# Gate and up of the small experts in two products of a joint high-low tile and a fold

## The chip, the cores and the metric

The kernel runs on one core of a Trainium2 chip. The metric is the device time of one execution in microseconds; the time before is the median of three runs. All times below are microseconds unless marked ns.

## The reference, cut to what matters

A two-layer hybrid block (latent attention, retention, block attention, then a dense feed-forward in layer 0 and eight routed experts in layer 1) is followed by a second block (feed-forward, gated mixing, cross attention, feed-forward), all in float32, on 256 tokens of width 1024. The change lies in the eight experts:

```python
def swiglu(x, w_gate, w_up, w_down):
    return (jax.nn.silu(x @ w_gate) * (x @ w_up)) @ w_down

def moe_swiglu(x, w_router, w_gate, w_up, w_down):      # D_MODEL 1024, D_FF_EXPERT 3584, N_EXPERTS 8, TOP_K 2
    ...
    y = jnp.zeros((B * S, D), jnp.float32)
    for e in range(N_EXPERTS):
        y = y + gates[:, e:e + 1] * swiglu(xt, w_gate[e], w_up[e], w_down[e]).astype(jnp.float32)
    return y.astype(x.dtype).reshape(B, S, D)
```

## The kernel before, in words

TensorE multiplies in a shortened float32 (fp32r). To keep float32 accuracy, every operand is split into a high part and a low part, and a product is made of three: high by high, high by low, low by high (`mm3`, L653 to L655). The weights come as a stream of chunks of 128 x 2048 float32 (1 MB). SyncE loads chunk n into one of six places of `raw` as soon as VectorE has split the chunk that stood there; ScalarE copies it to `whi` (the high part, `hi`, L1616); VectorE subtracts to get `wlo` (`lo`, L2134). `whi` and `wlo` have three homes each (`SPLIT`), so `hi` of chunk n waits until TensorE has used chunk n-3 (semaphore `used`).

In the expert stage each expert has the tokens that chose it, gathered as rows. Experts are sorted by their number of tokens; those at places 2, 4 and 6 (`FEW`) have at most 64 rows and are called small here, the others large. An expert's hidden width of 3584 is cut into 14 units of 256. A **slot** is one unit's gate and up (two chunks, 8 k-steps of 512 columns: 256 of gate and 256 of up) and the down projection (one chunk) of the slot before it, so down runs one slot late. Places 1 to 6 are worked in pairs: slots alternate between a large and a small expert. So 42 of the 112 slots are small ones.

In the texts below the three chunks of a small slot are **a** and **b** (gate and up of the small expert, k-steps 0 to 3 and 4 to 7) and **c** (down of the large unit before); those of a large slot are **d** and **e** (gate and up of the large expert) and **f** (down of the small unit before). A pair of slots is a b c d e f. Before the change, a, b, c, d and e take 12 products of 512 columns each, f takes 8: down of a small unit (`down_few`, L967 and L969) already uses a joint tile, with the high parts of 64 rows in columns 0 to 63 and the low parts in columns 64 to 127 of one 128-column operand, so that two products do for three and leave two halves of 64 rows that are added when the expert's sums are taken out (L1783, L1784 on ScalarE, L2403, L2405 on VectorE).

The order of the work on each engine is written out by hand:

- TensorE (`slot` in `experts`): gate and up of the slot, with two transposes of the former slot's gated unit (`turn`, L992) after k-step 1; in some slots four transposes that bring a later expert's rows into its lane (`turn_rows`, L940); then down of the former slot.
- ScalarE (`slot`): `hi` of the next slot's first chunk; wait for the end of gate and up; Silu of the gate half (L1796, written to `prob`); the lane copy (L1776) in gathering slots; `hi` of the next two chunks; the high part of the turned unit (L1814, `hth`).
- VectorE (`slot`): `lo` of the next slot's first chunk; gate by up (L2440); lane differences (L2395); `lo` of the next two chunks; the low part of the turned unit (L2461 for a small, L2464 for a large one, semaphore `e_ht`), for which down waits.

So `hi` and `lo` run for the slot ahead: during a large slot (d, e, f) they make a, b and c of the next small slot, and during a small slot d, e and f.

The lanes: a large expert's rows stand in `xth` (high) and `xtl` (low), a small expert's in `mem_hi` and `mem_lo`, the two halves of `mem_t`, 128 columns each, of which half are used. Slots whose code repeats were run in loops (`LOOPED`) on TensorE, ScalarE and VectorE.

Of the kernel before, what the change touches and what calls it, by code (L numbers as in the profile page):

```python
# [24 lines left out]
P = 128  # L25
# [32 lines left out]
SLOTS_FEW = P // 2  # L58
RANK_AT = (0, 1, 5, 2, 6, 3, 7, 4)
MIXED_AT = 8  # L60
GU_BANKS, TURNED_BEHIND = (0, 5), 1


def slot_of(e, j):

    if e == 0 or e == NE - 1:
        return U_E * e + j
    return U_E * (2 * ((e - 1) // 2) + 1) + 2 * j + (e - 1) % 2


SLOT = sorted(((e, j) for e in range(NE) for j in range(U_E)), key=lambda u: slot_of(*u))
GATED_AT, GATES_TURN_AT, X_SCALED_AT = slot_of(0, 6), slot_of(0, 8), slot_of(1, 7)
SHARES_AT, ROWS_BACK_AT = (slot_of(1, 6), slot_of(1, 8)), slot_of(1, 9)
GATHERS = {slot_of(0, 6): (1, 0), slot_of(0, 9): (1, 1), slot_of(0, 11): (2, 0), slot_of(0, 13): (2, 1)}
# [2 lines left out]
    for _g in range(2):  # L77
        GATHERS[slot_of(_beside, _j + _g)] = (_e, _g)
LOOPED = {slot_of(0, 2): 2, slot_of(NE - 1, 2): 2}
for _e in range(1, NE - 1, 2):  # L80
    LOOPED.update({slot_of(_e, 2): 3, slot_of(_e, 11): 2})
NEG = -1e30


# [193 lines left out]
def program(nc, stream, x_in, mem_in, pos_in, consts, route_in, cols_in, rows_in, ws_in, blank_in, out):  # L278
    with ExitStack() as ctx:
# [127 lines left out]
        def pair_columns(p, part, slot=0, heads=2):  # L407

            a = C_PAIR + W_PAIR * p + 2 * HD * part + HD * slot
            return slice(a, a + HD * heads)  # L410

        landed = [sem(f"landed{n}") for n in range(RAW)]
        hi_done = sem("hi_done")
        lo_done = sem("lo_done")
# [1 line left out]

        def lane(e):

            hi, lo = (mem_hi, mem_lo) if e in FEW else (xth, xtl)
            q = (e // 2 - 1) % 2 if e in FEW else (e + 1) // 2 % 2  # L420
            return hi, lo, slice(q * P, (q + 1) * P)

        def f32(ap):
            return ap.bitcast(F32)
# [225 lines left out]
        def _(pe):  # L650
# [270 lines left out]
            def experts():  # L921
# [18 lines left out]
                        m = pe.transpose(ps[4][:, k * P:(k + 1) * P], xs[:, (4 * g + k) * P:(4 * g + k + 1) * P], ident)  # L940
                    m.then_inc(sem("e_ga"), 1)

                def gate_up(e, bank, a, b, turned=None, first=False):
                    xh, xl, mine = lane(e)
                    for j, c in enumerate((a, b)):
                        chunk(c)
                        if first:
                            pe.wait_ge(sem("e_gx"), j + 1)
                        wh = whi[:, c.split, :].rearrange("p (k n) -> p k n", k=4)
                        wl = wlo[:, c.split, :].rearrange("p (k n) -> p k n", k=4)  # L950
                        for k in range(4):
                            kk = 4 * j + k
                            m = mm3(ps[bank][:, :], xh[:, kk, mine], xl[:, kk, mine],
                                    wh[:, k, :], wl[:, k, :], start=(kk == 0), stop=(kk == 7))
                            if kk == TURNED_BEHIND and turned is not None:
                                turn(turned)
                        m.then_inc(used, 1)

# [51 lines left out]
                def slot(s, it=0):  # L1010

                    e, j = SLOT[s]
                    u, base = s + 2 * it, first_chunk - 1 + 3 * s
                    if s == 0:
                        gate_up(e, GU_BANKS[0], Chunk(first_chunk), Chunk(first_chunk + 1), first=True)
                        return
                    if j == 0:
                        pe.wait_ge(sem("e_gx"), 2 * (e + 1))
                    if s == GATES_TURN_AT:
                        turn_gates()  # L1020
                    gate_up(e, GU_BANKS[s % 2], Chunk(base, it), Chunk(base + 1, it), u - 1)
                    if s in GATHERS:
                        if GATHERS[s] == (1, 1):
                            pe.wait_ge(sem("rt_spread"), 1)
                        turn_rows(*GATHERS[s])
                    done, n = SLOT[s - 1]
                    if n == 0 and done > 0:
                        pe.wait_ge(sem("e_oa"), done)
                        pe.wait_ge(sem("e_od"), done)
                    if s == 1:  # L1030
                        pe.wait_ge(*at("wk", "ev", 4))
                    if s == U_MOE - 1:
                        down(Chunk(base + 2), u - 1, done % 2, False, False, halves=(0,))
                        turn(u)
                        down(Chunk(base + 2), u - 1, done % 2, False, False, halves=(1,))
                        return
                    (down_few if done in FEW else down)(Chunk(base + 2, it), u - 1, done % 2, n == 0, n == U_E - 1)

                pe.wait_ge(sem("rt_one"), 1)
                pe.wait_ge(*at("wk", "ev", 2))  # L1040
                for g in range(2):
                    gather_first(g)
                keys(FILL["gather"])
# [558 lines left out]
        def _(act):  # L1602
# [167 lines left out]
            def experts():  # L1770
                first_chunk = AT["f1"]

                def gathered(e, g):
                    act.wait_ge(sem("e_ga"), 2 * e + g + 1)
                    xh, _, mine = lane(e)
                    act.activation(xh[:, 4 * g:4 * g + 4, mine], ps[4 + g if e == 0 else 4][:, :].rearrange("p (k s) -> p k s", k=4),  # L1776
                                   ACT.Copy).then_inc(sem("e_gh"), 1)

                def outputs(e, q, done):
                    act.wait_ge(sem("y_kept"), e + 1)  # L1780
# [7 lines left out]
                def slot(s, it=0):  # L1788

                    e, j = SLOT[s]  # L1790
                    few, final = e in FEW, s == U_MOE - 1
                    u, base = s + 2 * it, first_chunk - 1 + 3 * s
                    n = base + 3
                    hi(Chunk(n, it))
                    act.wait_ge(used, base + LB * it + 2 + (s == 0))
                    act.activation(sg[:, 0, :], ps[GU_BANKS[s % 2]][:, 0:FU], ACT.Silu).then_inc(sem("e_sg"), 1)  # L1796
                    if s == X_SCALED_AT:
                        act.wait_ge(sem("xg_in"), 16 * 2 * T)
                        for t in range(T):
                            act.activation(x[:, t, :], x[:, t, :], ACT.Copy, scale=float(ALPHA)).then_inc(sem("x_scaled"), 1)  # L1800
                    if s == GATES_TURN_AT:
                        act.wait_ge(sem("rt_turned"), 1)
                        act.activation(spread, ps[4][:, 0:S], ACT.Copy).then_inc(sem("rt_spread"), 1)
                    if s in GATHERS:
                        gathered(*GATHERS[s])
                    if final:
                        hi_half(Chunk(n + 1), 0)
                    else:
                        for i in (1, 2):
                            hi(Chunk(n + i, it))  # L1810
                    act.wait_ge(sem("e_ut"), u + 1)
# [10 lines left out]
                act.sem_inc(sem("e_oa"), 1)  # L1822
                for g in range(2):
                    gathered(0, g)
                advance(first_chunk + LEAD - 1)
# [290 lines left out]
        def _(dve):  # L2116
# [272 lines left out]
            def experts():  # L2389
                first_chunk = AT["f1"]  # L2390

                def gathered(e, g):
                    dve.wait_ge(sem("e_gh"), 2 * e + g + 1)
                    xh, xl, mine = lane(e)
                    dve.tensor_tensor(xl[:, 4 * g:4 * g + 4, mine], ps[4 + g if e == 0 else 4][:, :].rearrange("p (k s) -> p k s", k=4),  # L2395
                                      f32(xh[:, 4 * g:4 * g + 4, mine]), ALU.subtract).then_inc(sem("e_gx"), 1)

                def outputs(e, q, done):
# [30 lines left out]
                def slot(s, it=0):  # L2429
# [5 lines left out]
                    if final:  # L2435
                        lo_half(Chunk(n), 0)
                    else:
                        lo(Chunk(n, it))
                    dve.wait_ge(sem("e_sg"), u + 1)
                    dve.tensor_tensor(hs[:, 0, :], sg[:, 0, :], ps[GU_BANKS[s % 2]][:, FU:2 * FU], ALU.mult).then_inc(sem("e_h"), 1)  # L2440
                    if s in GATHERS:
# [10 lines left out]
                    if final:  # L2452
                        lo_half(Chunk(n), 1)
                    else:
                        for i in (1, 2):
                            lo(Chunk(n + i, it))
                    dve.wait_ge(sem("e_hh"), u + 1)
                    cut = slice(P, 2 * P) if final else slice(0, P)
# [784 lines left out]
```

## Time and profile before

| | |
|---|---|
| median of 3 runs | 2002.49 us |
| lowest and highest | 2001.07 and 2004.5 us |
| the profiled execution's own time | 2005.42 us |
| its span, first to last instruction | 2003.6 us |
| mean granted clock of TensorE | 0.996 |
| share of the span: PE, PEld, DVE, ACT, POOL | 98%, 81%, 75%, 62%, 4% |
| large and small slots in turn | from about 621 to 1298 us |

PE is TensorE, PEld its weight loads, DVE VectorE, ACT ScalarE, POOL GpSimd, SP SyncE. PE's busy share counts a product from its start to its modelled end; products overlap in the array, so that they start about 0.23 us apart although each lasts 0.39. An engine's row in the timeline gives the start, the length, the line and, in brackets, for how long the engine was idle before it and what released it.

### The profile page before, as it was taken

To read this page: it belongs to the slowest core of one execution; us is meant where nothing else is said; L and a number is where in the kernel's file an instruction comes from. 1 tells how busy PE (TensorE), PEld (TensorE's weight loads), DVE (VectorE), ACT (ScalarE), POOL (GpSimd) and SP (SyncE) were. 2 spreads that over 40 slices of the span, in tenths; PEclk is the share of its full clock that TensorE was granted. 3 is DMA by queue.
4 is the path that set the end of the run, shared out by engine and by line. 5 is a ranking of instruction groups with operands and counts; after the bars stand their busy time and mean duration, and the time that the engine had idled before them with its cause. 6 is when DMAs were issued, how large, how long until landed. Compare 5 with 4: busy or idle time off the path is not lost.

```text
span 2003.6 us, 25756 instructions
## 1 busy us (share of the span) xinstructions
PE 1959.0 (98%) x9454; PEld 1629.3 (81%) x9454; DVE 1502.3 (75%) x1573; ACT 1236.5 (62%) x1330; POOL 76.5 (4%) x96
## 2 busy tenths in 40 slices
PE   7999999999999999999999999999899999999998
PEld 6978887889788877888887888888688889888886
DVE  6685546777899989999999999999865556655554
ACT  5555444565777777777777777777644455535443
POOL 0002000001000000000000000010000012000000
PEclk9999999999999999999999999999999999999999
DMA  8348553436999999999999999999655545345550
GB/s 334 119 143 300 208 198 139 166 133 237 364 376 391 394 382 383 392 409 385 401 391 401 401 381 390 391 414 410 243 210 188 189 159 184 142 149 185 187 187 26
DMA packets 79663, 555.15 MB, mean 277 GB/s; under 512 B 8976, under 2 KB 9104, under 8 KB 17632
## 3 DMA queue, kind: packets, MB, share of 16 engines
q1 hardware_dynamic: 73728, 523.01, 68.1%
q0 software_dynamic: 5840, 30.85, 4.1%
q8 instruction: 63, 1.03, 0.2%
q14 instruction: 32, 0.26, 0.0%
HBM read 544.91 MB, written 12.58 MB: 278 GB/s over the span
## 4 chain that ended last, share of the span: by engine, by line
PE 90%; DVE 6%; ACT 2%; issue 1%; DMA 0%; POOL 0%; SPq 0%; ACTq 0%; DVEq 0%
PE ps L653 27%; PE ps L655 26%; PE ps L654 26%; DVE wlo L2134 3%; PE ps L967 2%; PE ps L969 2%; ACT whi L1616 1%; PE ps L992 1%; PE ps L864 1%; PE ps L1312 0%; PE ps L1288 0%; PE ps L1319 0%; PE ps L1188 0%; DMA bc<-in_rows 0%; PE ps L1168 0%
## 5 line engine op out<-in xcount | busy, mean ns | idle before, releaser
L2134 DVE TENSOR_TENSOR wlo<-raw,whi 128x2048 fp32r<-128x2048 f32 (+4 forms) x503 | 1132.3, 2260 | 273.5 <-ACT whi L1616 267.6
L1616 ACT ACTIVATE whi<-raw 128x2048 fp32r<-128x2048 f32 (+4 forms) x504 | 944.0, 1883 | 236.2 <-PE ps L655 225.5
L653 PE MATMUL ps<-whi,xth 128*128 128x512 f32 (+3 forms) x1504 | 598.5, 398 | 9.4 <-DVE wlo L2134 5.2
L655 PE MATMUL ps<-whi,xtl 128*128 128x512 f32 (+3 forms) x1504 | 580.2, 386 | 0.0
L654 PE MATMUL ps<-wlo,xth 128*128 128x512 f32 (+3 forms) x1504 | 578.6, 385 | 0.0
L653 PEld LDWEIGHTS ps<-whi,xth 128*128 128x128 f32 x1504 | 283.9, 189 | 67.1 <-DVE wlo L2134 12.0
L655 PEld LDWEIGHTS ps<-whi,xtl 128*128 128x128 f32 x1504 | 283.4, 188 | 55.2
L654 PEld LDWEIGHTS ps<-wlo,xth 128*128 128x128 f32 x1504 | 284.5, 189 | 49.0
L655 PE MATMUL ps<-whi,htl 128*128 128x512 f32 (+2 forms) x580 | 224.0, 386 | 0.0
L653 PE MATMUL ps<-whi,hth 128*128 128x512 f32 (+2 forms) x568 | 220.1, 387 | 0.0
L654 PE MATMUL ps<-wlo,hth 128*128 128x512 f32 (+2 forms) x568 | 219.1, 386 | 0.0
L653 PE MATMUL ps<-whi,mem_t 128*128 128x512 f32 x336 | 139.2, 414 | 2.1 <-DVE wlo L2134 2.0
L655 PE MATMUL ps<-whi,mem_t 128*128 128x512 f32 x336 | 132.0, 393 | 0.0
L654 PE MATMUL ps<-wlo,mem_t 128*128 128x512 f32 x336 | 131.5, 391 | 0.0
L655 PEld LDWEIGHTS ps<-whi,htl 128*128 128x128 f32 x580 | 108.9, 188 | 21.9
L654 PEld LDWEIGHTS ps<-wlo,hth 128*128 128x128 f32 x568 | 106.7, 188 | 20.9
L653 PEld LDWEIGHTS ps<-whi,hth 128*128 128x128 f32 x568 | 106.6, 188 | 21.0
L1796 ACT ACTIVATE prob<-ps 128x256 f32<-128x256 f32 x112 | 43.0, 384 | 93.8 <-PE ps L655 93.8
L653 PEld LDWEIGHTS ps<-whi,mem_t 128*128 128x128 f32 x336 | 63.0, 188 | 28.4 <-DVE wlo L2134 16.6
L655 PEld LDWEIGHTS ps<-whi,mem_t 128*128 128x128 f32 x336 | 63.0, 188 | 14.2
L1748 ACT ACTIVATE hth<-ps 128x512 fp32r<-128x512 f32 x30 | 18.0, 599 | 90.9 <-PE ps L864 90.9
L654 PEld LDWEIGHTS ps<-wlo,mem_t 128*128 128x128 f32 x336 | 63.3, 189 | 9.6
(436 smaller groups left out, 1678.6 us busy)
## 6 DMA issues: line engine op xcount, KB each, us to landing
raw<-in_stream SPq DMA_DIRECT2D x475, 1024.0 KB, 7.1
raw<-in_stream SPq DMA_DIRECT2D x16, 768.0 KB, 4.6
bc<-in_rows POOLq DMA_DIRECT2D x4, 1024.0 KB, 7.0
slot_rows<-in_blank POOLq DMA_DIRECT2D x7, 512.0 KB, 11.1
kc<-slot_rows POOLq DMA_DIRECT2D x7, 512.0 KB, 8.2
sum_rows<-r POOLq DMA_DIRECT2D x7, 512.0 KB, 8.5
raw<-in_stream SPq DMA_DIRECT2D x4, 832.0 KB, 6.7
raw<-in_stream SPq DMA_DIRECT2D x4, 640.0 KB, 3.9
```

The costliest lines, as they stand in the source:

```text
L653: pe.matmul(o, ah, bh, start=start, stop=False, skip_group_check=True)
L654: pe.matmul(o, ah, bl, start=False, stop=False, skip_group_check=True)
L655: return pe.matmul(o, al, bh, start=False, stop=stop, skip_group_check=True)
L864: m = pe.transpose(ps[2][:, k * S + t * P:k * S + (t + 1) * P], hs[:, t, k * P:(k + 1) * P], ident)
L967: pe.matmul(ps[2 + 4 * q + n][:, :], hth[:, k, 0:P], wh[:, k, cut], start=first and k == 0, stop=False, skip_group_check=True)
L969: m = pe.matmul(ps[2 + 4 * q + n][:, :], hth[:, k, 0:P], wl[:, k, cut], start=False, stop=last and k == 1, skip_group_check=True)
L992: m = pe.transpose(ps[1][:, k * P:(k + 1) * P], hs[:, 0, k * P:(k + 1) * P], ident)
L1616: act.activation(whi[:, c.split, 0:c.width], raw[:, c.raw, 0:c.width], ACT.Copy).then_inc(hi_done, 1)
L1748: act.activation(hth[:, 0:2, :], ps[2][:, :].rearrange("p (k s) -> p k s", k=2), ACT.Copy).then_inc(unit_sem(name, "hh"), 1)
L1796: act.activation(sg[:, 0, :], ps[GU_BANKS[s % 2]][:, 0:FU], ACT.Silu).then_inc(sem("e_sg"), 1)
L2134: dve.tensor_tensor(wlo[:, c.split, 0:c.width], raw[:, c.raw, 0:c.width], f32(whi[:, c.split, 0:c.width]), ALU.subtract).then_inc(lo_done, 1)
```

## The change

In a small slot the operand of gate and up is now one joint tile: the lane of 128 columns in `mem_hi` holds the high parts of the 64 rows in its first half and the low parts in its second. `gate_up_few` makes two products per k-step (joint tile by `whi`, joint tile by `wlo`) in place of three. The result bank then holds the high half's sums in rows 0 to 63 and the low half's in rows 64 to 127, which have to be added before the Silu: ScalarE copies rows 64 to 127 to an SBUF tile (`fold`, in `mem_end`), and TensorE adds them to rows 0 to 63 by a product with an identity of 64 x 64 (`fold_low`), placed behind the down projection c. The Silu waits for it. On ScalarE and VectorE `hi` and `lo` of the large slot's second chunk (e) move ahead of the Silu and of gate by up in small slots. The turn of a small unit, in the large slot behind it, comes after k-step 2 rather than 1. Lane copies and differences of small experts handle 64 rows rather than 128. The loops over pairs of slots are written out. The number of homes of the split weights stays at three.

```diff
-GU_BANKS, TURNED_BEHIND = (0, 5), 1
+GU_BANKS, TURNED_BEHIND, FEW_TURNED_BEHIND = (0, 5), 1, 2
...
-for _e in range(1, NE - 1, 2):
-    LOOPED.update({slot_of(_e, 2): 3, slot_of(_e, 11): 2})
...
+        fold_eye, fold = hth[0:SLOTS_FEW, 2, 0:SLOTS_FEW], mem_end[0:SLOTS_FEW, :, :].rearrange("p k s -> p (k s)")
...
+                def gate_up_few(e, bank, a, b, turned):
+                    both = slice(lane(e)[2].start, lane(e)[3].stop)
+                    for j, c in enumerate((a, b)):
+                        chunk(c)
...
+                        for k in range(4):
+                            kk = 4 * j + k
+                            pe.matmul(ps[bank][:, :], mem_hi[:, kk, both], wh[:, k, :], start=kk == 0, stop=False,
+                                      skip_group_check=True)
+                            m = pe.matmul(ps[bank][:, :], mem_hi[:, kk, both], wl[:, k, :], start=False, stop=False,
+                                          skip_group_check=True)
+                            if kk == TURNED_BEHIND:
+                                turn(turned)
+                        m.then_inc(used, 1)
+
+                def fold_low(bank, u):
+                    pe.wait_ge(sem("e_lowrows"), FEW_BEFORE[u] + 1)
+                    pe.matmul(ps[bank][0:SLOTS_FEW, :], fold_eye, fold, start=False, stop=True,
+                              skip_group_check=True).then_inc(sem("e_folded"), 1)
...
-                    gate_up(e, GU_BANKS[s % 2], Chunk(base, it), Chunk(base + 1, it), u - 1)
+                    if e in FEW:
+                        gate_up_few(e, GU_BANKS[s % 2], Chunk(base), Chunk(base + 1), u - 1)
+                    else:
+                        gate_up(e, GU_BANKS[s % 2], Chunk(base, it), Chunk(base + 1, it), u - 1,
+                                FEW_TURNED_BEHIND if SLOT[s - 1][0] in FEW else TURNED_BEHIND)
...
                     (down_few if done in FEW else down)(Chunk(base + 2, it), u - 1, done % 2, n == 0, n == U_E - 1)
+                    if e in FEW:
+                        fold_low(GU_BANKS[s % 2], s)
...
                     hi(Chunk(n, it))
-                    act.wait_ge(used, base + LB * it + 2 + (s == 0))
+                    if few:
+                        act.wait_ge(used, base + 2)
+                        act.activation(fold, ps[GU_BANKS[s % 2]][SLOTS_FEW:P, :], ACT.Copy).then_inc(sem("e_lowrows"), 1)
+                        hi(Chunk(n + 1))
+                        act.wait_ge(sem("e_folded"), FEW_BEFORE[s] + 1)
+                    else:
+                        act.wait_ge(used, base + LB * it + 2 + (s == 0))
                     act.activation(sg[:, 0, :], ps[GU_BANKS[s % 2]][:, 0:FU], ACT.Silu).then_inc(sem("e_sg"), 1)
...
-                        for i in (1, 2):
+                        for i in range(2 if few else 1, 3):
                             hi(Chunk(n + i, it))
...
                         lo(Chunk(n, it))
+                    if few:
+                        lo(Chunk(n + 1))
                     dve.wait_ge(sem("e_sg"), u + 1)
...
-                        for i in (1, 2):
+                        for i in range(2 if few else 1, 3):
                             lo(Chunk(n + i, it))
```

TensorE at the seam from a large to a small slot (ps2 and ps3 take down of a small unit, chunk f; ps5 takes gate and up of a small slot; ps1 takes the turn). Before:

```order
L969 MATMUL ps3<-wlo,hth 128x512
L653 MATMUL ps5<-whi,mem_t 128x512
L654 MATMUL ps5<-wlo,mem_t 128x512
L655 MATMUL ps5<-whi,mem_t 128x512
L653 MATMUL ps5<-whi,mem_t 128x512
L654 MATMUL ps5<-wlo,mem_t 128x512
L655 MATMUL ps5<-whi,mem_t 128x512
L992 MATMUL ps1<-cst,probt 128x128 x2
```

and with the change:

```order
L999 MATMUL ps3<-wlo,hth 128x512
L960 MATMUL ps5<-whi,mem_t 128x512
L962 MATMUL ps5<-wlo,mem_t 128x512
L960 MATMUL ps5<-whi,mem_t 128x512
L962 MATMUL ps5<-wlo,mem_t 128x512
L1022 MATMUL ps1<-cst,probt 128x128 x2
```

Each k-step of a small slot has lost its third product; the turn stands behind four products, not six.

TensorE at the seam from a small to a large slot with the change (ps7 takes the second half of down of a large unit, the end of chunk c; ps0 takes gate and up of the large slot, chunk d):

```order
L662 MATMUL ps7<-whi,hth 128x512
L663 MATMUL ps7<-wlo,hth 128x512
L664 MATMUL ps7<-whi,htl 128x512
L970 MATMUL ps5<-mem_end,hth 64x512
L662 MATMUL ps0<-whi,xth 128x512
L663 MATMUL ps0<-wlo,xth 128x512
L664 MATMUL ps0<-whi,xtl 128x512
```

The fold (L970, ps5) stands between c and d, where nothing stood before.

ScalarE through a large slot and the small slot behind it (prob is the Silu, hth the high part of the turned unit, mem_end the copied low rows; ps0 is the large, ps5 the small slot's bank). Before:

```order
L1616 ACTIVATE whi<-raw 128x2048
L1796 ACTIVATE prob<-ps0 128x256
L1616 ACTIVATE whi<-raw 128x2048 x2
L1814 ACTIVATE hth<-ps1 128x2x128
L1616 ACTIVATE whi<-raw 128x2048
L1796 ACTIVATE prob<-ps5 128x256
L1616 ACTIVATE whi<-raw 128x2048 x2
L1814 ACTIVATE hth<-ps1 128x2x64
```

and with the change:

```order
L1653 ACTIVATE whi<-raw 128x2048
L1839 ACTIVATE prob<-ps0 128x256
L1653 ACTIVATE whi<-raw 128x2048 x2
L1857 ACTIVATE hth<-ps1 128x2x128
L1653 ACTIVATE whi<-raw 128x2048
L1834 ACTIVATE mem_end<-ps5 64x512
L1653 ACTIVATE whi<-raw 128x2048
L1839 ACTIVATE prob<-ps5 128x256
L1653 ACTIVATE whi<-raw 128x2048
L1857 ACTIVATE hth<-ps1 128x2x64
```

In the small slot the copy of the low rows and one `hi` have come ahead of the Silu; the large slot's rows stand as they stood.

## Rows read from the trace of the kernel before

**Rows 1.** The page, part 1: busy time, share of the span, instructions

```profile
PE 1959.0 (98%) x9454; PEld 1629.3 (81%) x9454; DVE 1502.3 (75%) x1573; ACT 1236.5 (62%) x1330; POOL 76.5 (4%) x96
```

**Rows 2.** Busy: length, PE, PEld, DVE, ACT, POOL, PE clock, DMA share, GB/s

```profile
629.00:1298.00 669.00, 666.75 (x2993) 536.66 (x2992) 616.20 (x438) 518.30 (x428) 4.81 (x9) 1.00 0.99 393
1300.00:1400.00 100.00, 99.91 (x451) 81.56 (x450) 92.35 (x67) 76.13 (x64) 8.83 (x6) 1.00 1.01 413
```

**Rows 3.** Who waited for whom, 629 to 1298: us, times, longest

```profile
DVE wlo L2134 <- ACT whi L1616: 51.7, 150, 2.2
PEld ps L653 <- DVE wlo L2134: 17.6, 56, 2.0
...
PEld ps L653 <- issue: 0.7, 2, 0.4
```

**Rows 4.** Timeline of PE through one pair of slots: start, length, line, operation

```profile
868.03 0.39 PE L967 MATMUL ps<-whi,hth 128*128 128x512 f32 x1
...
869.86 0.50 PE L653 MATMUL ps<-whi,mem_t 128*128 128x512 f32 x1
870.20 0.39 PE L654 MATMUL ps<-wlo,mem_t 128*128 128x512 f32 x1
...
875.69 0.39 PE L653 MATMUL ps<-whi,hth 128*128 128x512 f32 x1
...
878.41 0.39 PE L653 MATMUL ps<-whi,xth 128*128 128x512 f32 x1
...
879.54 0.40 PE L655 MATMUL ps<-whi,xtl 128*128 128x512 f32 x1
879.77 0.39 PE L992 MATMUL ps<-cst,probt 128*128 128x128 f32 x2
879.91 0.47 PE L653 MATMUL ps<-whi,xth 128*128 128x512 f32 x1
880.23 0.39 PE L654 MATMUL ps<-wlo,xth 128*128 128x512 f32 x1
...
884.12 0.39 PE L967 MATMUL ps<-whi,hth 128*128 128x512 f32 x1
```

**Rows 5.** Timeline of ACT in the same pair

```profile
868.23 0.38 ACT L1796 ACTIVATE prob<-ps 128x256 f32<-128x256 f32 x1 [0.74 <-PE ps L655]
868.51 3.71 ACT L1616 ACTIVATE whi<-raw 128x2048 fp32r<-128x2048 f32 x2
```

**Rows 6.** Timeline of DVE in the same pair

```profile
867.52 2.29 DVE L2134 TENSOR_TENSOR wlo<-raw,whi 128x2048 fp32r<-128x2048 f32 x1 [0.44 <-ACT whi L1616]
...
870.45 4.50 DVE L2134 TENSOR_TENSOR wlo<-raw,whi 128x2048 fp32r<-128x2048 f32 x2 [0.31 <-ACT whi L1616]
874.86 0.42 DVE L2464 TENSOR_TENSOR htl<-ps,hth 128x256 fp32r<-128x256 f32 x1
```

**Rows 7.** Timeline of PE, ACT and DVE: a pair with more work for ACT

```profile
735.43 0.39 PE L967 MATMUL ps<-whi,hth 128*128 128x512 f32 x1
...
735.91 2.00 ACT L1800 ACTIVATE resid<-resid 128x1024 f32<-128x1024 f32 x2
...
744.15 0.42 DVE L2464 TENSOR_TENSOR htl<-ps,hth 128x256 fp32r<-128x256 f32 x1
...
753.37 0.39 PE L967 MATMUL ps<-whi,hth 128*128 128x512 f32 x1
```

**Rows 8.** Groups by line and shape: busy us, mean ns, idle before

```profile
L1783 ACT ACTIVATE r<-ps 64x512 f32<-64x512 f32 x3 | 1.8, 597 | 0.1
...
L1776 ACT ACTIVATE mem_t<-ps 128x512 fp32r<-128x512 f32 x6 | 3.6, 599 | 0.3
...
L1814 ACT ACTIVATE hth<-ps 128x256 fp32r<-128x256 f32 x70 | 25.9, 370 | 1.0 <-PE ps L992 1.0
```

**Rows 9.** Timeline of DVE where a small expert's sums are taken out

```profile
858.67 0.67 DVE L2403 TENSOR_TENSOR r<-ps,r 64x512 f32<-64x512 f32 x1
859.27 0.67 DVE L2405 TENSOR_TENSOR r<-ps,r 64x512 f32<-64x512 f32 x1
```

More of the change, by code:

```diff
@@ L71 @@
 SLOT = sorted(((e, j) for e in range(NE) for j in range(U_E)), key=lambda u: slot_of(*u))
+FEW_BEFORE = [sum(_e in FEW for _e, _ in SLOT[:_s]) for _s in range(U_MOE)]
 GATED_AT, GATES_TURN_AT, X_SCALED_AT = slot_of(0, 6), slot_of(0, 8), slot_of(1, 7)
@@ L417, in lane, with rows_of @@
         def lane(e):
-            hi, lo = (mem_hi, mem_lo) if e in FEW else (xth, xtl)
-            q = (e // 2 - 1) % 2 if e in FEW else (e + 1) // 2 % 2
-            return hi, lo, slice(q * P, (q + 1) * P)
+            if e in FEW:
+                a = (e // 2 - 1) % 2 * P
+                return mem_hi, mem_hi, slice(a, a + SLOTS_FEW), slice(a + SLOTS_FEW, a + P)
+            a = (e + 1) // 2 % 2 * P
+            return xth, xtl, slice(a, a + P), slice(a, a + P)
+        def rows_of(e):
+            return SLOTS_FEW if e in FEW else P
         def f32(ap):
@@ L941, in turn_rows, with gate_up @@
                     m.then_inc(sem("e_ga"), 1)
-                def gate_up(e, bank, a, b, turned=None, first=False):
-                    xh, xl, mine = lane(e)
+                def gate_up_few(e, bank, a, b, turned):
+                    both = slice(lane(e)[2].start, lane(e)[3].stop)
+                    for j, c in enumerate((a, b)):
+                        chunk(c)
+                        wh = whi[:, c.split, :].rearrange("p (k n) -> p k n", k=4)
+                        wl = wlo[:, c.split, :].rearrange("p (k n) -> p k n", k=4)
+                        for k in range(4):
[11 more added lines that the diff above has]
+                              skip_group_check=True).then_inc(sem("e_folded"), 1)
+                def gate_up(e, bank, a, b, turned=None, behind=TURNED_BEHIND, first=False):
+                    xh, xl, mine, mine_low = lane(e)
                     for j, c in enumerate((a, b)):
@@ L952, in gate_up @@
                             kk = 4 * j + k
-                            m = mm3(ps[bank][:, :], xh[:, kk, mine], xl[:, kk, mine],
+                            m = mm3(ps[bank][:, :], xh[:, kk, mine], xl[:, kk, mine_low],
                                     wh[:, k, :], wl[:, k, :], start=(kk == 0), stop=(kk == 7))
-                            if kk == TURNED_BEHIND and turned is not None:
+                            if kk == behind and turned is not None:
                                 turn(turned)
@@ L1037, in slot @@
                     (down_few if done in FEW else down)(Chunk(base + 2, it), u - 1, done % 2, n == 0, n == U_E - 1)
+                    if e in FEW:
+                        fold_low(GU_BANKS[s % 2], s)
                 pe.wait_ge(sem("rt_one"), 1)
                 pe.wait_ge(*at("wk", "ev", 2))
+                pe.wait_ge(sem("fold_eye"), 1)
                 for g in range(2):
@@ L1774, in gathered @@
                     act.wait_ge(sem("e_ga"), 2 * e + g + 1)
-                    xh, _, mine = lane(e)
-                    act.activation(xh[:, 4 * g:4 * g + 4, mine], ps[4 + g if e == 0 else 4][:, :].rearrange("p (k s) -> p k s", k=4),
-                                   ACT.Copy).then_inc(sem("e_gh"), 1)
+                    xh, _, mine, _ = lane(e)
+                    turned = ps[4 + g if e == 0 else 4][:, :].rearrange("p (k s) -> p k s", k=4)
+                    act.activation(xh[:, 4 * g:4 * g + 4, mine], turned[:, :, 0:rows_of(e)], ACT.Copy).then_inc(sem("e_gh"), 1)
                 def outputs(e, q, done):
@@ L1822, in experts @@
                 act.sem_inc(sem("e_oa"), 1)
+                act.activation(fold_eye, ident[0:SLOTS_FEW, 0:SLOTS_FEW], ACT.Copy).then_inc(sem("fold_eye"), 1)
                 for g in range(2):
@@ L2393, in gathered @@
                     dve.wait_ge(sem("e_gh"), 2 * e + g + 1)
-                    xh, xl, mine = lane(e)
-                    dve.tensor_tensor(xl[:, 4 * g:4 * g + 4, mine], ps[4 + g if e == 0 else 4][:, :].rearrange("p (k s) -> p k s", k=4),
+                    xh, xl, mine, mine_low = lane(e)
+                    turned = ps[4 + g if e == 0 else 4][:, :].rearrange("p (k s) -> p k s", k=4)
+                    dve.tensor_tensor(xl[:, 4 * g:4 * g + 4, mine_low], turned[:, :, 0:rows_of(e)],
                                       f32(xh[:, 4 * g:4 * g + 4, mine]), ALU.subtract).then_inc(sem("e_gx"), 1)
```

## The prediction, made before the changed kernel was run

> **What bounds the kernel now.** First the page's busy times: PE is busy for 98% of the span [rows 1], so fewer products look like time saved. But PE's busy share also counts overlap, so the second view is the busy time by stretch, for the stretch in which large and small slots alternate, 629 to 1298 [rows 2]: PE 666.8 of 669, VectorE 616.2, the DMA engines 0.99 busy at 393 GB/s. Three engines are near their ends there; VectorE has only 52.8 left. Third, the waits in that stretch [rows 3]: VectorE is idle for 51.7, waiting for ScalarE's high parts, and PE's weight loads already wait 56 times, 17.6 in all, for VectorE's low parts. So PE is first by a hair, and the question is what is second.
>
> The timeline of one pair of slots answers it [rows 4 to 6]. I follow the work that must be done in turn. PE begins chunk f at 868.03; gate and up of the large slot have just ended, so ScalarE's Silu runs at 868.23 and then `hi` of b and of c from 868.51, since both stand behind the Silu on ScalarE [rows 5]. VectorE has `lo` of b and c from 870.45, 4.50 for the two, and behind them the low part of the turned unit, from 874.86 to 875.28 [rows 6]. Chunk c needs that low part. From f to there: 875.28 - 868.03 = **7.25**. PE begins c at 875.69, 0.41 later, because b is only then done. c takes until 878.41 (12 products, 2.72), d and e until 884.12 (5.71), where the next f begins [rows 4]. One pair: 7.25 + 0.41 + 2.72 + 5.71 = **16.09**. That is PE's own work too (68 products at 0.227 and two turns), so two loops have nearly one length: PE's, and the loop Silu - `hi` - `lo` - `lo` - low part - c - d - e, with 0.41 to spare. A pair in which ScalarE has 2.00 of other work behind the Silu shows it [rows 7]: from f (735.43) to the low part's end (744.57) 9.14, to the next f (753.37) 17.94. The pair grew by 1.85 where the inner chain grew by 1.89: nothing absorbs a delay there.
>
> **The change, part by part.** *Products.* A small slot loses 8 of 24 products, 4 in a and 4 in b. 42 slots x 8 = 336 products at 0.227 = 76 of PE's time. But a and b lie beside the inner chain, not in the loop: what releases c is the 7.25, and it has no product of a or b in it. Now a starts at 869.86 as before and ends after 8 products and the turn at about 872.0; b must wait for its `lo`, done at 870.45 + 2.29 = 872.74, and its 8 products end at 874.7. c then waits for the low part until 875.28. So the gain is the 0.41 and no more; the rest becomes waits of PE ahead of b and c, some 0.7 and 0.6 in a pair.
>
> *c after a wait.* VectorE's end to PE's start takes 0.05 (867.52 + 2.29 = 869.81, PE at 869.86), and the first product after a wait holds the next back: 0.34 between the two starts (869.86, 870.20), not 0.23 [rows 4, 6]. So c is 2.72 + 0.11 = 2.83.
>
> *The fold* is one product of 64 x 64 by 512 columns between c and d, so it is in the loop 42 times. Everything hangs on its price. No row shows a product of that shape. Below, a product of 512 columns in a stream: 0.23. Above, nothing overlapped: two products end to end last 0.39 each [rows 4], 0.16 more at each seam, and both seams' weights loaded late besides. In between stands the nearest row, the turn: its way in costs nothing (879.54 to 879.77, 0.23), its way back holds the second product 0.09 late (879.91 to 880.23, 0.32). The turn has the full 128 x 128 shape of its neighbours; the fold has not, so I count a late load on both sides, 0.05 for its own 64 columns and 0.10 for d's 128. I take 0.23 + 0.15 = **0.38**.
>
> *New period*: 7.25 + 0.05 + 2.83 + 0.38 + 5.71 = **16.22**, against 16.09: +0.13. With the fold at price p it is 15.84 + p.
>
> *ScalarE and VectorE.* The copy of the low rows costs 0.60 (64 x 512 out of PSUM [rows 8]). It starts when b ends, 0.4 ahead of c's release, and PE needs it only 2.8 after that: hidden under c; without that cover it would add up to 0.60 a pair. Queued behind it are `hi` of e and, behind the wait for the fold, the Silu and `hi` of f. `hi` of e ends about 2.1 behind c's release, just when VectorE, done with `lo` of d, wants it. `lo` of d and e end 4.4 behind it, gate by up at 4.8, and the turn in d, behind 9 products, wants that at 3.26 + 2.04 = 5.3: 0.5 to spare, bought by the move of the turn behind k-step 2. f needs its `lo` and low part at about 9.0; they are ready near 8. The next a ties with its `lo`, but has 0.7 to spare ahead of b. In the large slot ScalarE's and VectorE's order is as it was, so the 7.25 stays.
>
> *Lane copies.* Of the small experts' six, four fall where a large slot's Silu is followed by the copy (L1776). 256 elements instead of 512: 0.60 to about 0.37 [rows 8], and this is in the inner chain: 4 x -0.23 = -0.9.
>
> *Sums taken out.* Twice a small expert's sums (two additions, 0.60 apart, 1.2 in all [rows 9]) push `lo` of d and e back in a small slot. 0.5 is covered; before, part of it was covered too. Between 0 and 1.2 each; I take 0.4: +0.8.
>
> *Loops written out.* Waits for issue are 0.7 in the whole stretch [rows 3]: nothing to gain. The identity's copy ahead of the stage comes while ScalarE waits: nothing.
>
> Sum: 42 x 0.13 = +5.5, -0.9, +0.8: **+5.4**. The profiled execution would have a span of 2009.0 for 2003.6; its own time, 2005.4, is 2.9 above the median of the runs, so the median goes from 2002.5 to **2007.9**.
>
> **The rivals.** *The fold drains the array.* If d's first product can't start before the fold has ended, nor the fold before c's last product has, each seam costs 0.39 - 0.23 = 0.16 more: p = 0.70, period 16.54, +0.45 x 42 = +18.9, **2021**. It needs only that the 64 x 64 shape is a different setting of the array. For it: nothing in the trace has that shape. Against: the turn's way in is free. The Trainium skill, "TensorEngine Tiling (Array Packing)", section Key Properties, says that a change of tiling mode drains TensorE; the rows here show no such change, so no row bears it out or refutes it. By that rule the time is this rival's, by the turn's row my forecast.
>
> *The fold is an ordinary product*: p = 0.23, period 16.07, -0.02 x 42 = -0.8, **2001.6**: no change. For it: 12 products in a row follow each other at 0.227 whatever their weights [rows 4].
>
> *Faster, a little.* c's first product is not late and the fold costs 0.21: 15.94, -6, **1996**. *Faster, much.* The inner chain is not what holds c, and a pair falls to what its engines can do: VectorE 616.2 / 41 pairs = 15.0, the DMA engines 6.29 MB at the 413 GB/s of the last large expert [rows 2] 15.2; -0.9 x 42 = -37, **1965**. Against: ScalarE's order in the large slot would have to be another, and rows 7 show the chain binding.
>
> *It saves products but not where it says*: the 76 of PE do go away, and must show up as PE's waits; this is part of the forecast, not a case of its own.
>
> **How the numbers follow.** A measurement of this kernel can tell about 0.2%, 4.0, from no change: faster is below 1998.5, slower above 2006.5. Forecast, p from 0.30 to 0.46, 2004.5 to 2011: 0.42, of which 0.12 below 2006.5. Ordinary fold, 2000.7 to 2004.5: 0.24. Draining fold, 2011 to 2025: 0.20. A little faster: 0.09; much: 0.05. So slower 0.30 + 0.20 = 0.50, same 0.24 + 0.12 = 0.36, faster 0.14. The range goes from 1998 to 2020: it leaves out the faster cases but for a rest, 0.12, and the upper part of the draining fold, 0.07.
>
> **What would show it.** In the profile after: the third product on `mem_t` (336 rows) gone; PE's idle time in the stretch up from 2 to some 60, released by VectorE's `lo` ahead of b and by the low part (L2464's successor) ahead of c; f to f 16.1 to 16.3 in a plain pair, f to the low part's end still 7.25; the seam c - fold - d at 0.38 above what it was. A seam of 0.7 is the draining fold. I am wrong if c starts well after the low part's end, if f to the low part is no longer 7.25, or if the turn in d waits for gate by up.

## The result, and the profile after

The changed kernel takes 2023.33 (median of 4 runs, 2020.89 to 2023.51), the kernel before 2003.49 in the same comparison: 1.0097 times as long, with a 95% interval of 1.0085 to 1.0109. It is slower by about 19.8; 2007.9 was forecast, with a range up to 2020. The medians here and below leave out two disturbed executions, of 5414.62 (f3) and of 2802.38 (the kernel before).

The page of the profile after, part 1, as in [rows 1]: busy time, share of the span, instructions.

```profile
PE 1924.8 (95%) x9160; PEld 1563.4 (77%) x9160; DVE 1497.1 (74%) x1573; ACT 1255.8 (62%) x1373; POOL 76.5 (4%) x96
```

294 products fewer (336 gone, 42 folds added). The busy time by stretch, as in [rows 2], for the alternating slots: length, PE, PEld, DVE, ACT, POOL, clock, DMA share, GB/s.

```profile
629.00:1310.00 681.00, 630.53 (x2686) 470.71 (x2685) 606.45 (x435) 533.19 (x466) 4.27 (x8) 1.00 0.98 382
```

PE was idle for 2 of 669 and is idle for 50 of 681. Who waited for whom in that stretch, as in [rows 3] (us in total, times, longest):

```profile
DVE wlo L2178 <- ACT whi L1653: 74.0, 117, 2.2
...
PEld ps L960 <- DVE wlo L2178: 55.4, 70, 2.9
...
PE ps L960 <- DVE wlo L2178: 29.9, 41, 2.5
...
PE ps L662 <- DVE htl L2511: 20.1, 39, 0.5
...
PEld ps L970 <- issue: 14.1, 40, 0.4
...
PEld ps L662 <- issue: 11.2, 40, 0.9
```

PE waits once in each pair ahead of b, for VectorE's low part of the weights (L960, 29.9 in 41 waits, 0.7 each in the mean), and once ahead of c, for the low part of the turned unit (L2511, 20.1 in 39 waits, 0.5 each). The last two rows are the seams of the fold: weight loads that wait for nothing the profile shows, 0.35 each in the mean ahead of the fold (L970) and 0.28 ahead of d (L662).

The timeline of PE through one pair, as in [rows 4]: start, length, line, operation. The first and the last row are the first products of f; the row at 878.57 is the first of c, 881.18 the last of c, 881.50 the fold, 881.87 the first of d.

```profile
871.17 0.39 PE L997 MATMUL ps<-whi,hth 128*128 128x512 f32 x1
...
875.94 0.51 PE L960 MATMUL ps<-whi,mem_t 128*128 128x512 f32 x1 [0.60 <-DVE wlo L2178]
...
878.57 0.47 PE L662 MATMUL ps<-whi,hth 128*128 128x512 f32 x1 [0.52 <-DVE htl L2511]
...
881.18 0.39 PE L664 MATMUL ps<-whi,htl 128*128 128x512 f32 x1
881.50 0.45 PE L970 MATMUL ps<-mem_end,hth 64*64 64x512 f32 x1
881.87 0.50 PE L662 MATMUL ps<-whi,xth 128*128 128x512 f32 x1
882.21 0.39 PE L663 MATMUL ps<-wlo,xth 128*128 128x512 f32 x1
...
887.67 0.39 PE L997 MATMUL ps<-whi,hth 128*128 128x512 f32 x1
```

ScalarE and VectorE in the same pair, as in [rows 5, 6]:

```profile
871.37 0.39 ACT L1839 ACTIVATE prob<-ps 128x256 f32<-128x256 f32 x1 [0.76 <-PE ps L664]
871.65 3.71 ACT L1653 ACTIVATE whi<-raw 128x2048 fp32r<-128x2048 f32 x2
```

```profile
873.59 4.49 DVE L2178 TENSOR_TENSOR wlo<-raw,whi 128x2048 fp32r<-128x2048 f32 x2 [0.32 <-ACT whi L1653]
878.00 0.42 DVE L2511 TENSOR_TENSOR htl<-ps,hth 128x256 fp32r<-128x256 f32 x1
```

From f to the end of the low part: 878.42 - 871.17 = 7.25, as before. From there to c 0.15; c with the way into the fold 2.93; the fold and the way to d 0.37; d and e 5.80. Together 16.50 for a plain pair, 16.09 before. Over the 42 pairs the stretch grew from 686.0 to 703.6, by 17.6 (from the Silu of slot 14 to that of slot 98 in both traces). The spans of these two executions differ by 15.5 only (2003.6 and 2019.1), because the stretch begins 3.4 earlier in the one after; the first Silu of the experts lies between 497.8 and 502.3 in the traces of all the runs, so that is scatter. The 17.6 lies in the interval of the medians' difference, 17.0 to 21.8.

### The profile page after: what moved, and what is told of

Same layout as the page of the kernel before. It is cut to its first block, busy times and chain, and to the rows that moved or that the text cites. A ratio compares the mean times of both kernels' runs of the same rounds, so it can differ in the third digit from the quotient of the medians.

```text
span 2019.1 us, 24773 instructions
## 1 busy us (share of the span) xinstructions
PE 1924.8 (95%) x9160; PEld 1563.4 (77%) x9160; DVE 1497.1 (74%) x1573; ACT 1255.8 (62%) x1373; POOL 76.5 (4%) x96
## 4 chain that ended last, share of the span: by engine, by line
PE 76%; DVE 16%; ACT 6%; issue 2%; DMA 0%; POOL 0%; SPq 0%; ACTq 0%; DVEq 0%
PE ps L662 23%; PE ps L664 22%; PE ps L663 22%; DVE wlo L2178 12%; ACT whi L1653 5%; DVE htl L2511 1%; PE ps L970 1%; PE ps L1022 1%; PE ps L873 1%; PE ps L1325 0%; PE ps L1349 0%; PE ps L1356 0%; DMA bc<-in_rows 0%; PE ps L1225 0%; PE ps L1205 0%
## 5 line engine op out<-in xcount | busy, mean ns | idle before, releaser
L662 PE MATMUL ps<-whi,xth 128*128 128x512 f32 (+3 forms) x1504 | 602.7, 401 | 8.9 <-DVE wlo L2178 5.4
L662 PEld LDWEIGHTS ps<-whi,xth 128*128 128x128 f32 x1504 | 283.7, 189 | 74.3 <-issue 13.3
L662 PE MATMUL ps<-whi,hth 128*128 128x512 f32 (+2 forms) x568 | 224.0, 394 | 21.5 <-DVE htl L2511 21.5
L960 PE MATMUL ps<-whi,mem_t 128*128 128x512 f32 x336 | 144.3, 429 | 29.9 <-DVE wlo L2178 29.9
L662 PEld LDWEIGHTS ps<-whi,hth 128*128 128x128 f32 x568 | 106.6, 188 | 57.5 <-DVE wlo L2178 34.7
L663 PEld LDWEIGHTS ps<-wlo,hth 128*128 128x128 f32 x568 | 106.8, 188 | 19.8
L960 PEld LDWEIGHTS ps<-whi,mem_t 128*128 128x128 f32 x336 | 63.6, 189 | 66.1 <-DVE wlo L2178 55.6
L997 PE MATMUL ps<-whi,hth 128*128 128x512 f32 x168 | 66.4, 395 | 0.0
L999 PE MATMUL ps<-wlo,hth 128*128 128x512 f32 x168 | 65.5, 390 | 0.0
```

The source lines that it names most:

```text
L662: pe.matmul(o, ah, bh, start=start, stop=False, skip_group_check=True)
L663: pe.matmul(o, ah, bl, start=False, stop=False, skip_group_check=True)
L960: pe.matmul(ps[bank][:, :], mem_hi[:, kk, both], wh[:, k, :], start=kk == 0, stop=False, skip_group_check=True)
L997: pe.matmul(ps[2 + 4 * q + n][:, :], hth[:, k, 0:P], wh[:, k, cut], start=first and k == 0, stop=False, skip_group_check=True)
L999: m = pe.matmul(ps[2 + 4 * q + n][:, :], hth[:, k, 0:P], wl[:, k, cut], start=False, stop=last and k == 1, skip_group_check=True)
```

## The experiments

The theory: a pair of slots lasts as long as the loop Silu - `hi` of b - `lo` of b - `lo` of c - low part - c - fold - d - e; the saved products lie beside it, the fold and its seams in it. (A seam is the passage from one product to the next of another kind.) In the table, a pair is the median of the 42 distances from one Silu to the Silu two slots later; the ratios are to the kernel before, with 95% intervals.

| kernel | median us | ratio | pair |
|---|---|---|---|
| before | 2003 to 2005 | | 16.11 |
| the change | 2023.33 | 1.0097 (1.0085 to 1.0109) | 16.52 |
| e1: no fold | 1998.87 | 0.9970 (0.9959 to 0.9980) | 15.94 |
| e2: fold of 128 x 128 | 2009.26 | 1.0020 (1.0010 to 1.0030) | 16.16 |
| e3: two folds | 2033.41 | 1.0143 (1.0121 to 1.0165) | 16.77 |
| e4: before with two products | 1998.72 | 0.9976 (0.9966 to 0.9987) | 15.95 |
| e5: before, loops written out | 2004.96 | 1.0008 (0.9998 to 1.0018) | 16.12 |
| e6: fold of 64 rows x 128 columns | 2024.75 | 1.0097 (1.0080 to 1.0114) | 16.57 |
| e7: fold of 128 rows x 64 columns | 2008.95 | 1.0020 (1.0010 to 1.0029) | 16.19 |
| e8: fold on VectorE | 2001.16 | 0.9981 (0.9971 to 0.9990) | 15.94 |
| f1: the change, four homes | 1983.95 | 0.9906 (0.9886 to 0.9927) | 15.54 |
| f2: before, four homes | 1995.98 | 0.9964 (0.9953 to 0.9976) | 15.97 |
| f3: the change, four homes, full fold | 1980.11 | 0.9881 (0.9857 to 0.9904) | 15.40 |

**e1, the fold taken out.**

```diff
-                    if e in FEW:
-                        fold_low(GU_BANKS[s % 2], s)
...
-                        act.wait_ge(sem("e_folded"), FEW_BEFORE[s] + 1)
+                        act.wait_ge(used, base + 3)
```

> The changed kernel without the fold's product: the copy of the low rows stays, the Silu waits for the end of chunk c instead, so the low half's sums are never added (that part of gate and up is left out). Theory (the loop Silu - hi - lo - lo - low part - c - fold - d - e sets the pair, and the fold with its two seams costs 0.57 in it): c to d follow in stream, pair 7.25 + 0.15 + 2.84 + 5.71 = 15.95 instead of 16.50, -23, about 2000. Rival (the moved hi and lo of e, or the copy, hold the loop up): the pair stays above 16.3, the time above 2015.

Measured: 1998.87, pair 15.94. PE through one pair, the first products of f, c, d and the next f:

```profile
866.92 0.39 PE L997 MATMUL ps<-whi,hth 128*128 128x512 f32 x1
...
874.32 0.47 PE L662 MATMUL ps<-whi,hth 128*128 128x512 f32 x1 [0.52 <-DVE htl L2509]
...
877.12 0.39 PE L662 MATMUL ps<-whi,xth 128*128 128x512 f32 x1
...
882.80 0.39 PE L997 MATMUL ps<-whi,hth 128*128 128x512 f32 x1
```

c to d is 2.80, d and e 5.68, the pair 15.88 here. The copy, the move of `hi` and `lo` of e, the later turn and the written-out loops are all still there: the whole loss against before, and 0.58 of a pair in the median (16.52 to 15.94), is the fold's product with its seams. Three of the 42 pairs do not fit this; they stand with the smaller terms below.

**e4, the saved products alone**, on the kernel before.

```diff
-                            m = mm3(ps[bank][:, :], xh[:, kk, mine], xl[:, kk, mine],
-                                    wh[:, k, :], wl[:, k, :], start=(kk == 0), stop=(kk == 7))
+                            if e in FEW:
+                                pe.matmul(ps[bank][:, :], xh[:, kk, mine], wh[:, k, :], start=kk == 0, stop=False,
+                                          skip_group_check=True)
+                                m = pe.matmul(ps[bank][:, :], xh[:, kk, mine], wl[:, k, :], start=False, stop=kk == 7,
+                                              skip_group_check=True)
+                            else:
+                                m = mm3(ps[bank][:, :], xh[:, kk, mine], xl[:, kk, mine],
+                                        wh[:, k, :], wl[:, k, :], start=(kk == 0), stop=(kk == 7))
```

> The kernel before with the third product (whi by the low rows) of gate and up left out in small slots, nothing else touched: no copy, no fold, loops and the order of hi and lo as before. Theory (the saved products lie beside the loop): pair 15.95 for 16.06 to 16.09, -4 to -6 against before, about 1998. Rival (PE's time is what counts): 336 x 0.227 = -76, about 1927.

Measured: 1998.72, pair 15.95. 336 products of 0.227, 76 of PE's time, are worth 0.24% (0.13 to 0.34), some 5 us. That is as much as in e1: with nothing added, the products bring no more than the slack of 0.41 less the late start of c.

**e2, the fold in the full shape.** The weights are 128 x 128 with zeros around the 64 x 64 identity, the lower 64 moving rows zero.

```diff
-                    pe.matmul(ps[bank][0:SLOTS_FEW, :], fold_eye, fold, start=False, stop=True,
+                    pe.matmul(ps[bank][:, :], fold_eye, fold_all, start=False, stop=True,
```

> The changed kernel with the fold in the full shape: 128 x 128 weights, of which only the 64 x 64 identity is not zero, and 128 rows moving, of which the lower 64 are zero. Same sums. Theory (the 64 x 64 shape is what makes the seams dear): the fold costs 0.23 as in a stream, seams of 0.34 together go, pair 16.16, -14, about 2009. Rival (any product between c and d with its own wait costs that much): pair 16.4 to 16.5, above 2018.

**e3, the small fold twice.**

```diff
+                    pe.matmul(ps[bank][0:SLOTS_FEW, :], fold_eye, fold, start=False, stop=False,
+                              skip_group_check=True)
                     pe.matmul(ps[bank][0:SLOTS_FEW, :], fold_eye, fold, start=False, stop=True,
```

> The changed kernel with the fold's product made twice in a row in the same 64 x 64 shape (the low rows are added twice, so the sums are off). Theory (seams cost, not the product): +0.23 a pair, +10, about 2033. Rival (every product of this shape costs 0.57): +24, about 2047.

**e6 and e7, one side of the shape at a time.** As e2, but `fold_eye[0:SLOTS_FEW, :]` by `fold` (64 rows, 128 columns), and `fold_eye[:, 0:SLOTS_FEW]` by `fold_all` (128 rows, 64 columns).

> The fold with 64 rows moving but weights of 64 x 128 (columns 64 to 127 zero), so that only the number of rows differs from the products beside it. If the rows make the seams dear: pair 16.4 to 16.5, about 2022 as the change. If the columns do: pair 16.15, about 2009 as the full shape. If each has a share: between, 16.25 to 16.4.

> The fold with all 128 rows moving (64 of them zero) and weights of 128 x 64, so that only the number of columns differs from the products beside it. If the columns make the seams dear: pair 16.4 to 16.5, about 2022. If the rows do: pair 16.15, about 2009.

Their times stand in the table. The seam in the trace of each, PE from the last product of c over the fold to d: e2:

```profile
876.50 0.39 PE L665 MATMUL ps<-whi,htl 128*128 128x512 f32 x1
876.73 0.39 PE L971 MATMUL ps<-mem_end,hth 128*128 128x512 f32 x1
876.96 0.39 PE L663 MATMUL ps<-whi,xth 128*128 128x512 f32 x1
877.18 0.39 PE L664 MATMUL ps<-wlo,xth 128*128 128x512 f32 x1
```

e3:

```profile
871.45 0.39 PE L664 MATMUL ps<-whi,htl 128*128 128x512 f32 x1
871.77 0.45 PE L970 MATMUL ps<-mem_end,hth 64*64 64x512 f32 x1
872.06 0.40 PE L972 MATMUL ps<-mem_end,hth 64*64 64x512 f32 x1
872.38 0.50 PE L662 MATMUL ps<-whi,xth 128*128 128x512 f32 x1
872.72 0.40 PE L663 MATMUL ps<-wlo,xth 128*128 128x512 f32 x1
```

e6:

```profile
883.94 0.39 PE L665 MATMUL ps<-whi,htl 128*128 128x512 f32 x1
884.26 0.50 PE L971 MATMUL ps<-mem_end,hth 64*128 64x512 f32 x1
884.68 0.50 PE L663 MATMUL ps<-whi,xth 128*128 128x512 f32 x1
885.02 0.39 PE L664 MATMUL ps<-wlo,xth 128*128 128x512 f32 x1
```

e7:

```profile
880.03 0.39 PE L665 MATMUL ps<-whi,htl 128*128 128x512 f32 x1
880.26 0.40 PE L971 MATMUL ps<-mem_end,hth 128*64 128x512 f32 x1
880.49 0.39 PE L663 MATMUL ps<-whi,xth 128*128 128x512 f32 x1
880.72 0.40 PE L664 MATMUL ps<-wlo,xth 128*128 128x512 f32 x1
```

The weight loads of the fold and of d, in the change:

```profile
881.50 0.13 PEld L970 LDWEIGHTS ps<-mem_end,hth 64*64 64x64 f32 x1 [0.35 <-issue]
881.87 0.19 PEld L662 LDWEIGHTS ps<-whi,xth 128*128 128x128 f32 x1 [0.24 <-issue]
```

and in e7:

```profile
880.03 0.13 PEld L971 LDWEIGHTS ps<-mem_end,hth 128*64 128x64 f32 x1
880.26 0.19 PEld L663 LDWEIGHTS ps<-whi,xth 128*128 128x128 f32 x1
```

With 128 rows (e2, e7) the starts follow each other at 0.23, as in any stream: the fold costs 0.23. With 64 rows they stand 0.32, 0.37 and 0.34 apart in the change (1.03 for three), 0.32, 0.42 and 0.34 in e6 (1.08): 0.34 and 0.40 above a stream. The second fold of e3 adds 0.24 to the seam and 10.1 to the time (2033.41 - 2023.33): a second product of the small shape costs a product, so the cost is in going from 128 rows to 64 and back. That it is the rows and not the columns was open between e6 and e7, and they settle it. The wait for the copied rows is not the cost: e2 and e7 have it too. The weight loads show where the time goes: with 128 rows the fold's begins 0.22 to 0.23 ahead of its product (all 42 pairs of e2 and of e7, and d's in 40 of each), with 64 rows the fold's and d's begin only together with theirs (all 42 pairs of the change and of e6). What holds them back is not shown. The times follow: e2 and e7 save 14 of the change's 20, e6 none.

**e8, the fold on VectorE**, which adds the copied rows in the bank between `lo` of d and `lo` of e; the turn of a small unit comes a k-step later.

```diff
+                        dve.tensor_tensor(ps[GU_BANKS[s % 2]][0:SLOTS_FEW, :], ps[GU_BANKS[s % 2]][0:SLOTS_FEW, :], f32(fold),
+                                          ALU.add).then_inc(sem("e_folded"), 1)
```

> The changed kernel with the fold made by VectorE (it adds the copied low rows to rows 0 to 63 in the bank, between lo of d and lo of e, about 0.67) in place of TensorE's product, and the turn of a small unit one k-step later. Theory: the addition lies beside the loop, so the pair is that without a fold, 15.95 to 16.0, about 1999 to 2002, a little below before; VectorE's need rises to 15.6, still below. Rival (VectorE's own time is on the path in small slots too): 16.3 and more, above 2013.

Measured: 2001.16, pair 15.94, a little faster than before. VectorE in one small slot: the low part that releases c, `lo` of d, the addition, `lo` of e.

```profile
873.54 0.42 DVE L2512 TENSOR_TENSOR htl<-ps,hth 128x256 fp32r<-128x256 f32 x1
873.87 2.28 DVE L2176 TENSOR_TENSOR wlo<-raw,whi 128x2048 fp32r<-128x2048 f32 x1
876.07 0.68 DVE L2484 TENSOR_TENSOR ps<-ps,mem_end 64x512 f32<-64x512 f32 x1
876.67 2.27 DVE L2176 TENSOR_TENSOR wlo<-raw,whi 128x2048 fp32r<-128x2048 f32 x1
```

From 629 to 1290 VectorE is busy for 629 of 661 there, PE for 613. 0.60 more of the busier engine costs nothing, since it comes behind the low part, where VectorE is ahead of its use; 0.57 of PE between c and d costs its full length in a plain pair. What counts is the place in the loop, not the engine's load.

**f1, a fourth home for the high parts of the weights** in the alternating slots. It stands in the tile of two rows of the last norm, whose load moves behind the stage. In large slots `hi` of b, which no longer waits for the end of e, goes ahead of the Silu; `lo` of b waits for e instead.

```diff
+FOUR_FROM, FOUR_TO = AT["f1"] + 3 * 16, AT["f1"] + 3 * 97
+HIGH = [_n % 4 if FOUR_FROM <= _n < FOUR_TO else _n % SPLIT for _n in range(NCHUNK)]
...
                     hi(Chunk(n, it))
+                    if early:
+                        hi(Chunk(n + 1))
...
+                if c.freed < c.base - SPLIT + 1:
+                    dve.wait_ge(used, c.n - SPLIT + 1)
```

> The changed kernel with a fourth home for the high part of the weights in the alternating slots (in the place of two rows that are needed only later and are now loaded later), and, in large slots, hi of b ahead of the Silu, since it no longer waits for the end of e. lo of b waits for the end of e instead. Theory (it is this loop that holds the pair): Silu and hi of b leave the loop, 7.25 falls by about 1.4, and the next bounds are VectorE's 15.0 and the DMA engines' 15.2 a pair: pair 15.2 to 15.6, -38 to -55 against the change, 1968 to 1985. Rival (the pair is held by something the loop shares, such as the DMA engines at 393 GB/s): pair above 16.2, above 2010.

Measured: 1983.95, pair 15.54. PE through one pair (f, c, the fold, the next f):

```profile
872.76 0.39 PE L1013 MATMUL ps<-whi,hth 128*128 128x512 f32 x1
...
879.17 0.47 PE L678 MATMUL ps<-whi,hth 128*128 128x512 f32 x1 [0.54 <-DVE htl L2532]
...
882.09 0.45 PE L986 MATMUL ps<-mem_end,hth 64*64 64x512 f32 x1
...
888.29 0.39 PE L1013 MATMUL ps<-whi,hth 128*128 128x512 f32 x1
```

f to c is 6.41, in the change 7.40; the rest is 9.12 (9.10 there). The loop lost 0.99 and the pair 0.97: it was the loop that held it. The fall is less than the 1.4 expected, since c still waits for the low part; VectorE works without a gap ahead of it, from 869.26, where `lo` of a had waited 1.04 for ScalarE, to 879.03. The rival does not hold the pair: ScalarE waits for no load of weights in that stretch.

**f2, the same fourth home in the kernel before**, loops written out.

> The kernel before with the same fourth home and the same move of hi of b, loops written out. Theory: PE's own 68 products and two turns a pair, 16.05, are the bound there, so plain pairs stay at 16.0 to 16.1 and only those in which ScalarE or VectorE have other work gain: -2 to -5, about 1999. Rival (the fourth home is worth as much without the saved products): as much as in the changed kernel, 30 and more below before.

Measured: 1995.98, pair 15.97, 0.36% below before (0.24 to 0.47), some 7; expected were 2 to 5. It is a little more, because the small waits of [rows 3] go too (plain pairs fall to 15.95, below the 16.0 expected), but it is a fifth of the 39 that the same home brings in the changed kernel. With three products a k-step, PE itself is the bound (it is idle for 1.4 of 656 in f2, from 629 to 1285); with two, the loop is, and then opening it pays. In f1 and f2 the last of the 42 pairs, where the fourth home ends, is some 2 longer than the others (18.1 and 18.3); why is not shown.

**f3, four homes and the full fold.** The two edits together.

> The changed kernel with the fourth home and the fold in the full 128 x 128 shape. Theory: with the loop open PE's 14.7 a pair is below VectorE's and the DMA engines' needs, so the cheaper fold, worth 14 with three homes, is worth less than 5 here: 1965 to 1985, within 5 of the one with the small fold. Rival (PE is the bound with four homes): 14 below it.

Measured: 1980.11, 0.9881 of before (0.9857 to 0.9904): this version beats both. The stretch of 629 to 1270 in its trace, columns as above:

```profile
629.00:1270.00 641.00, 613.68 (x2699) 479.57 (x2698) 603.01 (x436) 529.99 (x468) 4.81 (x9) 1.00 1.00 410
```

VectorE is busy for 603 of 641 and the DMA engines move 410 GB/s, near the 413 of [rows 2]; the cheaper fold is worth some 4 here by the medians, 6 by the same stretch of the two traces (666.0 and 659.8 for the 42 pairs), against 14 with three homes. Less than 5 was expected; that it is much less than 14 fits the theory.

**e5, the loops written out** in the kernel before, by leaving out the two lines of `LOOPED` that the change leaves out.

> The kernel before with the loops over pairs of slots written out, as the change does, and nothing else. Theory: no row shows a wait for instructions there, so within 2 of before. Rival (written-out code costs or gains fetch time): more than 4 off.

Measured: 2004.96, 1.0008 (0.9998 to 1.0018): nothing.

## Why the prediction was wrong

*What bounds the kernel* was right, for a plain pair. f to the low part is 7.25 in both traces; the products saved turned into PE's waits ahead of b and c (0.7 and 0.5 in a pair, 0.7 and 0.6 forecast); e4 gives their worth by themselves, and e8 and f1 show the loop by putting work beside it and by opening it.

*The step that failed is the price of the fold*, taken at 0.38. It is 0.57: 0.23 for the product, 0.09 on the way in (0.32 between the starts), 0.14 on the way out (0.37) and 0.11 for d's first product (0.34 to the next). I had counted 0.05 and 0.10 for late weight loads, by the turn's rows, which have the full shape. The loads are late, as counted, but the seams come to 0.34, not 0.15. 42 x 0.19 = 8.0.

*The second term that was too small is the start of c*: 0.15 behind the end of the low part, not 0.05. I took 0.05 from a row in which PE waits for `lo`; where it waits for the low part of the turned unit it takes three times as long, in the change as in e1 (874.32 there). Why is not shown. 42 x 0.10 = 4.2.

For a plain pair the account closes: the period of 16.22 becomes 16.22 + 0.19 + 0.10 = 16.51; the trace has 16.50. That 8.0 and 4.2 on top of the +5.4 forecast are the stretch's 17.6 to the tenth is partly luck, since smaller terms that were off nearly cancel.

*The rival of the draining fold* (0.70 a pair for the fold, 2021) came nearest in time. It was given 0.20, with its reason against it from the turn's way in; that row could not speak for a shape that it does not have. Its working was not quite what the trace shows: the fold starts at 881.50, before the end of c's last product (881.18 + 0.39), and d before the end of the fold, by the profile's ends, which are modelled. The seams cost 0.34 between them, the rival's own terms came to 0.47. The Trainium skill, "TensorEngine Tiling (Array Packing)", section Key Properties, has TensorE drain at a change of tiling mode. Where the rows change, the trace agrees that a change costs (0.34 and 0.40 in the change and in e6); where the columns alone change (e7), it shows no cost, and there the measurement decides (if such a product changes the mode at all, which no run shows).

*The smaller terms.* Plain pairs grew by 0.33 to 0.52, 0.44 in the median. Lane copies of 64 rows: the four pairs with such a copy grew by 0.20 to 0.25 (16.73 to 16.93 for one), so about -0.2 each holds. Sums taken out: the two such pairs grew by 0.42 and 0.37 (16.52 and 16.57 to 16.94), but not by the fold: they last 16.94 to 16.96 without it (e1), with the full or the half shape (e2, e6, e7) and with two (e3). There VectorE, which works from 856.66 to 869.80 without a gap in the first of them, holds the pair, and PE's turn in d waits for gate by up, one of the forecast's own signs of being wrong. So the +0.4 each came, but in place of the fold's price and not on top of it. The pair of [rows 7], with ScalarE's extra work, grew by 1.10 (17.94 to 19.04), 0.66 more than a plain one; that was not forecast. It is 18.55 in e4 and 18.64 in e1, which have no fold, and 18.05 in e2, so the fold does not explain it, and the cause stays open. Loops written out: nothing, as forecast (e5). The copy of the low rows stayed hidden in plain pairs (e1 has it, e4 has not, and both have 15.9).

*The range* ended at 2020 because the draining case was cut at its upper part. With a term that stands in the loop 42 times and has no row of its kind, the end should have been the upper bound's, 2021 and more.

## What to carry to other kernels

When an engine is busy for nearly the whole of a stretch (here 667 of 669) and the next for 92% of it, write down the loop from a buffer's release to its next use and add it up: work that is saved beside that loop becomes waiting, and anything put into it is paid in full, however idle its engine looks, wherever that loop is what holds the work. An operation of a shape that no row has should be priced by its upper bound until measured; and if it can take the shape of its neighbours (zeros around it), that may be the cheaper form, as here by 14 us. Saving and opening the loop belong together: the products saved brought 5 us alone, the fourth home 7 alone, both with the full fold 1.2%.

## What the runs showed of the hardware

A product with 64 contraction rows between products with 128 cost 0.57 to 0.63 instead of 0.23, the second of two in a row about 0.24; a product with 64 columns of weights and 128 rows cost 0.23, like its neighbours. With 64 rows the weight loads of that product and of the next began together with the product, with 128 rows 0.22 ahead. After a wait for the low part of the turned unit, PE started 0.14 to 0.15 behind the end of the instruction that released it (41 pairs of the change), after a wait for `lo` 0.05 ([rows 4, 6]). PE's granted clock stayed at 1.00, the upper of its two levels of 1.2 and 2.4 GHz, through the whole stretch although PE now waited twice in nearly every pair, 0.7 and 0.5 in the mean and once 2.5.
